# Squaring the input two adaLN rows earlier, with GpSimd summing the squares, and zeros copied from DRAM

## The chip, the cores and the metric

The kernel runs on one core of a Trainium2 chip. The core has five engines with instruction streams of their own: TensorE (PE in the rows, PEld its weight loads, PEq its sequencer), VectorE (DVE), ScalarE (ACT), GpSimd (POOL) and SyncE (SP). They meet only through semaphores. DMAs are issued by SP, ACT and POOL and are carried out by 16 DMA engines. The metric is the device time of one execution, in microseconds (us), the median of several runs.

## The reference

One inference step of a two-layer backbone, batch 1: 128 context tokens and 256 latent tokens (T = 384) of width D = 1024, in float32. Ahead of each sub-layer stands an adaLN norm; both token kinds have their own shift, scale and gate, which come from a conditioning vector and one large matrix:

```
mod = silu(cond) @ w_ada[l] + b_ada[l]        # 6 x D columns: sh1 sc1 gt1 sh2 sc2 gt2
h   = rms_norm(x, g) * (1 + sc) + sh          # rms_norm: x * rsqrt(mean(x^2) + eps) * g
```

Layer 0 then projects `h` to the inputs of a Mamba-2 scan (16 heads) and of latent attention (8 heads); layer 1 to grouped-query attention (16 heads). Each layer ends with a mixture of 16 experts, top 2 per token. The kernel returns the tokens and the new states and caches.

## The kernel before

Everything lies transposed: `xT` and `hT` are 128 partitions x 8 chunks (DC) x 384 tokens, chunk c holding channels 128c to 128c+127. Weights come in 114 slots of 128 x 3072 floats (1536 KB each, `w_d`), which SP loads one after the other into a ring of 8 buffers (L384); a buffer is loaded anew when its user has counted `slot_used` up. The order of the slots is the order of use: 6 of the first layer's adaLN (N_FIRST), 7 of the first input projection (INE), the other 26 adaLN slots that are used here and there up to the attention, the output projection, the experts. SP puts the input `xT` behind the third slot (L386) and the constants `small` (3147.5 KB, the rest of them; the first 192 KB go by ACT's queue at the very start) behind the sixth (L388). The first 8 slots wait for nothing, so all of this is queued in the first microseconds and lands in this order.

The order of work on each engine is written out by hand. The start of the program is this:

- PE, `ada(n)` for n = 0 to 5 (L438): row n of the adaLN product, 8 matmuls with a 32-column weight (16 passes in the trace, since each float32 matmul shows as two). ACT copies the row out (`copy_row`, L1028), and PE turns it into columns (`turn_row`, L450: 3 matmuls of 2 columns, 6 passes), one row behind. After row 5 both remaining rows are turned, and `ada_done` is set.
- Ahead of row 5, ACT squares the 8 chunks of x into hT (L895), PE sums them over channels with 8 matmuls against a matrix of ones (`sum_squares`, L466), ACT takes the root (L878, with a table load), and DVE the reciprocal (L1239).
- DVE adds the bias to the turned columns (`modulation`, L1233), forms g * (1 + scale) (L1246), and scales the 8 chunks in 16 instructions (L1251); ACT adds the shift (L906), chunk by chunk; PE's next matmuls take the chunks as they come (`h_chunk`).
- These next matmuls are `dk` (L677): a 48-column projection that gives dt and the rotary key. Its weights are in `small`. Then come the INE slots (L474), 8 matmuls (16 passes) for each of 13 column chunks and then for the z parts; behind column chunk 0 PE turns `dk` (`dkT`, L690), which DVE copied out. ACT and DVE run the convolution on chunks 0 to 9 in PE's shadow.
- GpSimd fills the DRAM table of expert rows (8192 rows of 4 KB) with zeros: it clears 1024 columns of the SBUF region `oTm` (L1663), waits for the eighth scaled chunk (`h_scaled`), and issues 16 DMAs of 2048 KB from there (L1667). `oTm` is later overwritten by the scan, so DVE waits for `row_cleared` ahead of the scan. GpSimd waits for it too, ahead of its sums for the second norm (`sum_chunks`, L1658), in which it adds squares of chunks 0 to 6 on the way, so that PE needs two matmuls instead of eight. That scheme is used for the norms ahead of the experts only. The small outputs kpe and ckv go by GpSimd's queue behind the zeros, and ACT and DVE wait for them at the start of the latent attention.

PSUM results go through 5 banks in turn, in the order of a list of jobs; a job's bank must have been emptied five jobs later.

Of the kernel before, what the change touches and what calls it, by code (L numbers as in the profile page):

```python
# [22 lines left out]
P = 128  # L23
D = 1024
# [16 lines left out]
N_ADA, N_INE, N_OUTE, N_MOE, N_INO, N_OUTO = 16, 7, 4, 32, 4, 3  # L41
S_ADA0 = 0
N_FIRST = 6
S_INE = S_ADA0 + N_FIRST
S_ADA_LATE = S_INE + N_INE
S_OUTE = S_ADA_LATE + 2 * N_ADA - N_FIRST
# [28 lines left out]
def build(nc, small_d, x_d, w_d, y_d, stf_d, stb_d, ckv_d, kpe_d, gk_d, gv_d):  # L75
# [7 lines left out]
    with ctx:  # L83
# [22 lines left out]
        def region(base, *widths):  # L106
# [14 lines left out]
        zs, xc, oTy, oTm, lat, dk, e_sm = region(0, 3072, CONV_C * 385, 3072, 1536, 1152, 144, 1000)  # L121
        TAIL = 3072 + CONV_C * 385 + 3072 + 1536 + 1152 + 144 + 1000
        rn, _, sq_acc = region(TAIL, 384, 116, 384)
        mod_row = [U[:, TAIL + 896:TAIL + 1280], U[:, TAIL + 500:TAIL + 884]]
        xr = [region(TAIL + 387 * i, 387)[0] for i in range(2)]
        zs3 = zs.rearrange("p (t n) -> p t n", t=NT)
# [73 lines left out]
            row_copied qkv_ready rt_exp flags_ready chosen_ready rows_ready cleared row_cleared scattered  # L200
# [40 lines left out]
        for l in range(DEPTH):  # L241
            job(("ss", l, 0), "A")
            if l == 0:
                job(("dk",), "D")
                for c in range(CONV_C):
                    job(("xbc", c), "A")
                    if c == 0:
                        job(("dkT",), "D")
                for c in range(3):
                    job(("lat", c), "D")  # L250
                for i in range(3):
                    for t in range(NT):
                        job(("z", i, t), "A")
                job(("cum",), "D")
                job(("tot",), "D")
                job(("sl", 0), "A")
                job(("sl", 1), "A")
                for i, (t, full) in enumerate(STEPS):
                    job(("xt", i, 0), "A")
                    job(("xt", i, 1), "A")  # L260
                    job(("bt", i), "A")
                    if full:
                        job(("g", i, 0), "A")
                        job(("g", i, 1), "A")
                        for u in range(8):
                            job(("bc", i, u), "D")
                        if t:
                            for d in range(2):
                                for g in range(2):
                                    job(("off", i, d, g), "D")  # L270
                        job(("yT", i, 0), "A")
                        job(("yT", i, 1), "A")
                    for d in STATES[i]:
                        job(("st", i, d), "D")
                for k in range(N_PREP + 1):
                    for hh in range(2):
                        if k < N_PREP:
                            job(("qkv", k, hh), "A")
                    for hh in range(2):
                        if k:  # L280
                            job(("qkT", k - 1, hh), "A")
                attention_jobs("mla", HM)
            else:
                for i in range(NT + 1):
                    for s in range(N_INO):
                        if i < NT:
                            job(("in", s, ORDER[i]), "A" if s % 2 else "D")
                    if i == 0:
                        job(("gkT", 3), "A")
                    if i:  # L290
                        job(("gqT", ORDER[i - 1], 0), "A")
                        job(("gqT", ORDER[i - 1], 1), "A")
                        job(("gkT", ORDER[i - 1]), "A")
                attention_jobs("gqa", HQ)
            for c in range(DC):
# [59 lines left out]
        def _(sp):  # L355
# [14 lines left out]
            for n in range(N_SLOTS):  # L370
# [13 lines left out]
                sp.dma_start(buffers[IN_BUFFER[n]], w_d[row_of_slot(n), :, :]).then_inc(slot_full[IN_BUFFER[n]], 16)  # L384
                if n == 2:
                    sp.dma_start(xT[:, :, :], x_d).then_inc(S["in_x"], 16)  # L386
                if n == N_FIRST - 1:
                    sp.dma_start(small[:, N_SMALL_FIRST:], small_d[:, N_SMALL_FIRST:]).then_inc(S["in_small"], 16)  # L388
            for c in (0, DC // 2):
                sp.wait_ge(S["x_new"], 3 * DC + c + DC // 2)  # L390
# [6 lines left out]
        def _(pe):  # L397
# [57 lines left out]

            def sum_squares(l, i):
                b = fill("ss", l, i)
                if i:
                    pe.wait_ge(S["sq_sum"], (DC - 2) * (l + 1))
                    mm(b[:, 0:T], ones, sq_acc, start=True, stop=False)  # L460
                    pe.wait_ge(S["sq_ready"], DC * (2 * l + 2))
                    filled(mm(b[:, 0:T], ones, hT[:, DC - 1, :], start=False, stop=True))
                    return
                for k in range(DC):
# [200 lines left out]

            pe.wait_ge(S["in_first"], 16)
            for n in range(N_FIRST):
                if n == N_FIRST - 1:
                    sum_squares(0, 0)
                ada(n)  # L670

            pe.wait_ge(S["in_small"], 16)
            wdk = sm("w_dk").rearrange("p (k n) -> p k n", k=DC)
            b = fill("dk")
            for k in range(DC):
                h_chunk(0, 0, k)
                ins = mm(b[0:48, 0:T], wdk[:, k, :], hT[:, k, :], start=(k == 0), stop=(k == DC - 1))  # L677
            filled(ins)
            for s in range(N_INE):
                w = slot(S_INE + s).rearrange("p (k n) -> p k n", k=DC)  # L680
                for m in range(3):
                    c = 3 * s + m
                    if c < 13:
                        b = fill("xbc", c) if c < CONV_C else fill("lat", c - CONV_C)
                        filled(project("in", b[:, 0:T], lambda k: w[:, k, P * m:P * m + P], lambda k: hT[:, k, :]))
                    if c == 0:
# [165 lines left out]
        def _(act):  # L852
# [34 lines left out]
                shift(l, i)  # L887

            def root_mean_square(l, i):
                for c in range(DC):  # L890
# [4 lines left out]
                    A(hT[:, c, :], xT[:, c, :], ACT.Square).then_inc(S["sq_ready"], 1)  # L895
                b = take("ss", l, i)
                root(rn, b[:, 0:T], D).then_inc(S["r_ready"], 1)
                act.wait_ge(S["r_ready"], 2 * l + i + 1)
# [133 lines left out]
                    copy_row(n)  # L1032

            for n in range(N_FIRST):
                if n == N_FIRST - 1:
                    root_mean_square(0, 0)
                copy_row(n)
            shift(0, 0)
            act.wait_ge(S["in_small"], 16)
# [153 lines left out]
        def _(dve):  # L1193
# [264 lines left out]
            normaliser(0, 0)  # L1458
            modulation(0)
            norm(0, 0)  # L1460
            dve.wait_ge(S["in_small"], 16)
# [6 lines left out]
            b = take("dk")  # L1468
            dve.tensor_copy(dk_f, b[0:48, 0:T]).then_inc(S["dk_by_feature"], 1)
            dve.wait_ge(S["dk_by_feature"], 1)  # L1470
            dve.sem_inc(S["free_dve"], 1)
            b = take("dkT")
            emptied_by(dve.tensor_copy(dk, b[:, 0:144]))
            dve.wait_ge(S["free_dve"], emptied[index[("dkT",)]][1])
            dve.sem_inc(S["dk_copied"], 1)
            cw = sm("conv_w")
            for c in range(CONV_C):
                dve.wait_ge(S["xr_ready"], c + 1)
                r, o = xr[c % 2], xc3[:, c, :]
                link(ts(o, r[:, 1:386], cw[:, CONV_C + c:CONV_C + c + 1], None, MUL))  # L1480
# [35 lines left out]
                ins = stt(latT[:, c, :], latT[:, c, :], g, lr[c // 2], MUL, MUL)  # L1516
            ins.then_inc(S["latn_ready"], 1)

            dve.wait_ge(S["row_cleared"], 16 * (NE * CAP // 512))
            nfull = 0  # L1520
            for i, (t, full) in enumerate(STEPS):
                dve.wait_ge(S["xtok_ready"], i + 1)
# [126 lines left out]

        @block.gpsimd  # L1650
        def _(pool):
            def sum_chunks(l):

                for c in range(1, DC - 1):
                    pool.wait_ge(S["sq_ready"], DC * (2 * l + 1) + c + 1)
                    if c > 1:
                        pool.wait_ge(S["sq_sum"], (DC - 2) * l + c - 1)
                    pool.tensor_tensor(sq_acc, hT[:, 0, :] if c == 1 else sq_acc, hT[:, c, :], ADD).then_inc(S["sq_sum"], 1)  # L1658

            def clear_rows():  # L1660

                zero = oTm[:, 0:D]
                pool.memset(zero, 0.0).then_inc(S["cleared"], 1)  # L1663
                pool.wait_ge(S["cleared"], 1)
                pool.wait_ge(S["h_scaled"], DC)
                for n in range(NE * CAP // 512):
                    pool.dma_start(rows_d[512 * n:512 * n + 512, :].rearrange("(p q) n -> p q n", q=4),  # L1667
# [2 lines left out]
            def moe(l):  # L1670
# [42 lines left out]
            sum_chunks(0)  # L1713
# [4 lines left out]
            sum_chunks(1)  # L1718
            moe(1)


# [96 lines left out]
```

## Time and profile before

| | us |
|---|---|
| median of 3 runs | 1145.91 |
| lowest and highest | 1140.90 and 1149.15 |
| the profiled execution | 1145.72 |
| its span in the trace | 1143.9 |

The page gives shares over the whole span: PE is busy 83% of it, DVE 33%, ACT 25%, POOL 4%. The change touches the first tenth of the span and one DMA stream, so those shares say little; the views to read are the timeline of the first 70 us, the chain of waits there, and the landing of single DMAs. In the rows, "x16" counts instructions merged into one row, the first column of a timeline or a chain is the start in us from the span's start, and the second the time in us.

### The profile page before, as it was taken

To read this page: it belongs to the slowest core of one execution; us is meant where nothing else is said; L and a number is where in the kernel's file an instruction comes from. 1 tells how busy PE (TensorE), PEld (TensorE's weight loads), DVE (VectorE), ACT (ScalarE), POOL (GpSimd) and SP (SyncE) were. 2 spreads that over 40 slices of the span, in tenths; PEclk is the share of its full clock that TensorE was granted. 3 is DMA by queue.
4 is the path that set the end of the run, shared out by engine and by line. 5 is a ranking of instruction groups with operands and counts; after the bars stand their busy time and mean duration, and the time that the engine had idled before them with its cause. 6 is when DMAs were issued, how large, how long until landed. Compare 5 with 4: busy or idle time off the path is not lost.

```text
span 1143.9 us, 14055 instructions
## 1 busy us (share of the span) xinstructions
PE 950.7 (83%) x5625; PEld 507.9 (44%) x5625; DVE 371.8 (33%) x924; ACT 290.7 (25%) x684; POOL 50.2 (4%) x63
## 2 busy tenths in 40 slices
PE   5999988786876699972999995898898963999994
PEld 2455655564643445532433334464544533323324
DVE  0332006655734471133111102345664151101112
ACT  1421023232333371031111110312665041101110
POOL 0310000000000000102000001000000102000002
PEclk8799998968988799986999998899789985999997
DMA  9999997532374401123599996406000216599934
GB/s 385 426 423 415 408 419 295 207 136 111 130 272 171 165 1 56 66 100 135 229 410 414 415 426 223 177 1 220 10 1 1 93 73 247 220 416 425 424 126 184
DMA packets 36339, 258.99 MB, mean 226 GB/s; under 512 B 3408, under 2 KB 3552, under 8 KB 21424
## 3 DMA queue, kind: packets, MB, share of 16 engines
q1 hardware_dynamic: 20448, 198.27, 43.3%
q0 software_dynamic: 12224, 47.01, 10.4%
q10 hardware_dynamic: 3600, 12.78, 2.8%
q8 instruction: 47, 0.77, 0.3%
q14 instruction: 20, 0.16, 0.0%
HBM read 203.17 MB, written 54.87 MB: 226 GB/s over the span
## 4 chain that ended last, share of the span: by engine, by line
PE 70%; DVE 12%; DMA 7%; ACT 6%; issue 3%; POOL 1%; SPq 0%; DVEq 0%; POOLq 0%; ACTq 0%
PE ps L474 20%; PE ps L586 13%; PE ps L608 7%; PE ps L828 6%; DMA U<-expert_rows 3%; PE ps L488 3%; PE ps L570 2%; PE ps L661 2%; PE ps L438 2%; DMA ring<-w_in 2%; PE ps L747 2%; PE ps L513 2%; PE ps L495 1%; PE ps L534 1%; DVE U L1538 1%
## 5 line engine op out<-in xcount | busy, mean ns | idle before, releaser
L586 PE MATMUL ps<-ring,U 128*32 128x512 f32 x1200 | 166.3, 592 | 0.0
L474 PE MATMUL ps<-U,ring 128*128 128x384 f32 x320 | 105.1, 487 | 2.7 <-DVE U L1317 1.4
L608 PE MATMUL ps<-ring,U 128*32 128x512 f32 x672 | 85.7, 594 | 0.0
L586 PEld LDWEIGHTS ps<-ring,U 128*32 128x32 f32 x1200 | 47.5, 110 | 85.3 <-issue 85.3
L474 PEld LDWEIGHTS ps<-U,ring 128*128 128x128 f32 x320 | 60.0, 189 | 47.4 <-issue 4.2
L586 PE MATMUL ps<-U 128*32 128x512 f32 x168 | 73.1, 592 | 0.0
L586 PE MATMUL ps<-hT,U 128*32 128x512 f32 x168 | 73.1, 592 | 0.0
L438 PE MATMUL ps<-ring,cond_w 128*32 128x384 f32 x512 | 59.5, 592 | 14.4 <-ACT cond_w L883 8.6
L828 PE MATMUL ps<-ring,hT 128*128 128x384 f32 x192 | 65.4, 501 | 5.7 <-ACT hT L906 4.9
L474 PE MATMUL ps<-hT,ring 128*128 128x384 f32 x208 | 68.6, 488 | 1.0 <-issue 1.0
L570 PE MATMUL ps<-small,U 128*128 128x128 f32 x192 | 31.7, 317 | 44.2 <-DMA U<-expert_rows 42.4
L1400 DVE TENSOR_TENSOR U<-ps,U 128x256 f32<-128x256 f32 x24 | 10.1, 422 | 134.7 <-ACT U L974 134.7
L474 PEld LDWEIGHTS ps<-hT,ring 128*128 128x128 f32 x208 | 39.0, 190 | 30.0 <-issue 4.0
L488 PE MATMUL ps<-U,hT 64*128 64x128 f32 (+3 forms) x144 | 50.0, 524 | 2.5 <-ACTq L924 1.1
L828 PEld LDWEIGHTS ps<-ring,hT 128*128 128x128 f32 x192 | 37.1, 196 | 33.1 <-issue 9.2
L570 PEld LDWEIGHTS ps<-small,U 128*128 128x128 f32 x192 | 24.4, 161 | 54.2 <-DMA U<-expert_rows 48.2
L895 ACT ACTIVATE hT<-xT 128x384 f32<-128x384 f32 x32 | 15.3, 517 | 129.5 <-DVE xT L1259 105.7
L1408 DVE COPY U<-ps 128x512 f32<-128x512 f32 x24 | 16.6, 692 | 91.6 <-PE ps L608 56.4
L661 PE MATMUL ps<-U 128*128 128x128 f32 x192 | 26.1, 306 | 23.5 <-DMA U<-expert_rows,U 23.5
L1259 DVE SCALAR_TENSOR_TENSOR xT<-ps,misc,xT 128x128 f32<-128x128 f32 (+1 forms) x32 | 11.9, 413 | 96.0 <-PE ps L474 96.0
L974 ACT ACTIVATE U<-ps 128x256 f32<-128x256 f32 x24 | 9.2, 385 | 131.2 <-PE ps L586 131.2
L474 PE MATMUL ps<-ring,hT 128*128 128x384 f32 (+1 forms) x144 | 42.0, 451 | 0.5 <-issue 0.5
(250 smaller groups left out, 1346.6 us busy)
## 6 DMA issues: line engine op xcount, KB each, us to landing
ring<-w_in SPq DMA_DIRECT2D x102, 1536.0 KB, 10.6
expert_rows<-U POOLq DMA_DIRECT2D x16, 2048.0 KB, 70.9
U<-expert_rows SPq DMA_DIRECT2D x24, 512.0 KB, 5.9
expert_rows<-U ACTq DMA_DIRECT2D x24, 512.0 KB, 9.0
hT<-w_in SPq DMA_DIRECT2D x6, 1536.0 KB, 12.2
U<-w_in SPq DMA_DIRECT2D x6, 1536.0 KB, 15.6
small<-small_in SPq DMA_DIRECT2D x1, 3147.5 KB, 34.1
xT<-x_in SPq DMA_DIRECT2D x1, 1536.0 KB, 16.7
```

Source lines behind the costliest of these rows:

```text
L438: ins = mm(ps[q:q + 32, bank_row, 0:384], cond3[:, k, :], w[:, k, :], start=(k < 4), stop=(k >= 4))
L474: ins = mm(out, lhs(k), rhs(k), start=(k == 0), stop=(k == n - 1))
L488: filled(mm(b[:, 0:nk], q_of(t, h), k_of(h, k0, nk), start=True, stop=True))
L513: ins = mm(ps[rows[i], 5 + pair % 2, P:T], v_of(1 + c, 2 * k + i), pt[i][:, P + 256 * c:P + 256 * c + 256], start=(c == 0), stop=(c == NT ...
L570: ins = pe.transpose(ps[:, 3 + h, P * c:P * c + P], xgb[i % NR][:, 512 * h + P * c:512 * h + P * c + P], ident)
L586: ins = mm(ps[q:q + 32, r, :], xgT[:, r, P * k + q:P * k + q + 32], w[e][:, c:c + 512], start=(k == 0), stop=(k == DC - 1))
L608: ins = mm(ps[q:q + 32, 6 + h, :], actT_of[i % NR][:, P * j + q:P * j + q + 32], w[e][:, c:c + 512], start=(j == 0), stop=(j == 1))
L661: ins = mm(ps[:, MIX_BANK[t] + h, P * c:P * c + P], picked[t][q][:, 512 * h + P * c:512 * h + P * c + P], gate_diag[q][t], start=(q == 0), ...
L747: ins = mm(ps[:, 5 + q // 2, 64 * hh:64 * hh + 64], dec[u % 3][:, P * h:P * h + P], xdt[d][:, 64 * (4 * q + h):64 * (4 * q + h) + 64], sta ...
L828: ins = mm(b[:, 0:384], hT[:, k, TILE[t]], w[:, k, :], start=(k == 0), stop=(k == DC - 1))
L895: A(hT[:, c, :], xT[:, c, :], ACT.Square).then_inc(S["sq_ready"], 1)
L1408: dve.tensor_copy(ysb[i % 2][:, 512:1024], ps[:, 7, :]).then_inc(S["y_dve"], 1)
```

## The change

1. ACT's root_mean_square(0, 0) is cut in two: the squares come ahead of `copy_row(3)`, the root ahead of `copy_row(4)`. PE's `sum_squares(0, 0)` moves from ahead of `ada(5)` to ahead of `ada(4)`.
2. The first norm uses GpSimd's sums as the expert norms do: GpSimd adds the squares of chunks 0 to 6 into `sq_acc0` (in the region oTy, free by then), six additions; PE does two matmuls.
3. SP loads the seventh slot (the first of INE) ahead of `small`.
4. `dk` moves behind column chunk 5 of INE, `dkT` behind chunk 6; the first INE column chunk now takes the chunks of h as they come. PE's wait for `small` moves along; DVE's moves behind the memsets of the convolution's edges; ACT's stays behind the shift.
5. The zeros are read from DRAM: the last output slot of layer 1 fills only 2048 of its 3072 columns, and the 1024 padded ones are the source. The memset and DVE's wait for `row_cleared` go.

```diff
+N_SQUARE = 3
+DK_AFTER = 5
...
+        sq_acc0 = oTy[:, 0:T]
...
-                if n == N_FIRST - 1:
+                if n == N_FIRST:
                     sp.dma_start(small[:, N_SMALL_FIRST:], small_d[:, N_SMALL_FIRST:]).then_inc(S["in_small"], 16)
...
             def sum_squares(l, i):
                 b = fill("ss", l, i)
-                if i:
-                    pe.wait_ge(S["sq_sum"], (DC - 2) * (l + 1))
-                    mm(b[:, 0:T], ones, sq_acc, start=True, stop=False)
-                    pe.wait_ge(S["sq_ready"], DC * (2 * l + 2))
+                if i or not l:
+                    pe.wait_ge(S["sq_sum"], (DC - 2) * (l + i + 1))
+                    mm(b[:, 0:T], ones, sq_acc if i else sq_acc0, start=True, stop=False)
+                    pe.wait_ge(S["sq_ready"], DC * (2 * l + i + 1))
...
             for n in range(N_FIRST):
-                if n == N_FIRST - 1:
+                if n == N_SQUARE + 1:
                     sum_squares(0, 0)
                 ada(n)
...
-            pe.wait_ge(S["in_small"], 16)
-            b = fill("dk")
-            for k in range(DC):
-                h_chunk(0, 0, k)
-                ins = mm(b[0:48, 0:T], wdk[:, k, :], hT[:, k, :], start=(k == 0), stop=(k == DC - 1))
-            filled(ins)
...
+                    if c == DK_AFTER:
+                        pe.wait_ge(S["in_small"], 16)
+                        b = fill("dk")
+                        filled(project("dk", b[0:48, 0:T], lambda k: wdk[:, k, :], lambda k: hT[:, k, :]))
+                    if c == DK_AFTER + 1:
                         pe.wait_ge(S["dk_by_feature"], 1)
...
             for n in range(N_FIRST):
-                if n == N_FIRST - 1:
-                    root_mean_square(0, 0)
+                if n == N_SQUARE:
+                    squares(0, 0)
+                if n == N_SQUARE + 1:
+                    root_of(0, 0)
                 copy_row(n)
...
-            dve.wait_ge(S["row_cleared"], 16 * (NE * CAP // 512))
...
-                zero = oTm[:, 0:D]
-                pool.memset(zero, 0.0).then_inc(S["cleared"], 1)
-                pool.wait_ge(S["cleared"], 1)
+                zero = w_d[S_OUTO + 2, :, 2 * D:SLOT]
...
+            sum_chunks(0, 0)
             clear_rows()
```

On PE, this is the start of the program from the fourth adaLN row on (`ring<-cond_w` rows are adaLN rows, `misc,U` the turns), before:

```order
L438 MATMUL ps<-ring,cond_w 32x384 x8
L450 MATMUL ps<-misc,U 128x2 x3
L438 MATMUL ps<-ring,cond_w 32x384 x8
L450 MATMUL ps<-misc,U 128x2 x3
L466 MATMUL ps<-hT,small 128x384 x8
L438 MATMUL ps<-ring,cond_w 32x384 x8
L450 MATMUL ps<-misc,U 128x2 x6
L677 MATMUL ps<-hT,small 48x384 x8
L474 MATMUL ps<-hT,ring 128x384 x8
```

And the same place now:

```order
L442 MATMUL ps<-ring,cond_w 32x384 x8
L454 MATMUL ps<-misc,U 128x2 x3
L464 MATMUL ps<-U,small 128x384
L466 MATMUL ps<-hT,small 128x384
L442 MATMUL ps<-ring,cond_w 32x384 x8
L454 MATMUL ps<-misc,U 128x2 x3
L442 MATMUL ps<-ring,cond_w 32x384 x8
L454 MATMUL ps<-misc,U 128x2 x6
L686 MATMUL ps<-hT,ring 128x384 x8
L478 MATMUL ps<-hT,ring 128x384 x40
L478 MATMUL ps<-hT,small 48x384 x8
```

Eight sum matmuls became two and stand one row earlier; the 48-column projection went behind 48 matmuls of the input projection.

On GpSimd, from its first own instruction to the outputs of layer 0 (U holds the zeros before; `ISA` ahead of an addition sets up the engine for it), before:

```order
L1663 MEMSET U 128x1024
L1667 DMA expert_rows<-U 512x1x1024 x16
L1706 DMA kpe_out<-U 128x32
L1708 DMA stf_out<-small 128x512
L1709 DMA stb_out<-small 128x512
L1711 DMA ckv_out<-U 128x128
L1658 ISA
L1658 TENSOR_TENSOR U<-hT 128x384
```

And now:

```order
L1675 ISA
L1675 TENSOR_TENSOR U<-hT 128x384
L1675 TENSOR_TENSOR U<-U,hT 128x384 x5
L1682 DMA expert_rows<-w_in 512x1x1024 x16
L1722 DMA kpe_out<-U 128x32
```

The additions and their set-up stand first, and the 16 zeroing DMAs now go from DRAM to DRAM.

## Rows read from the trace of the kernel before

**Rows 1.** The page: chain's share by engine, and DMA busy tenths in 40 slices.
```profile
PE 70%; DVE 12%; DMA 7%; ACT 6%; issue 3%; POOL 1%; SPq 0%; DVEq 0%; POOLq 0%; ACTq 0%
...
DMA  9999997532374401123599996406000216599934
```
**Rows 2.** Chain of waits in order of time, first 57 us: start, us, what.
```profile
3.06 19.72 DMA ring<-w_in
...
22.82 2.79 PE ps L438 x16
25.61 1.37 PE ps L450 x6
26.98 2.71 PE ps L438 x16
...
31.07 7.37 PE ps L466 x16
...
39.05 2.57 DVE U L1239
...
41.64 0.21 DVE misc L1233
...
43.81 7.80 PE ps L677 x16
51.61 5.36 PE ps L474 x16
```
**Rows 3.** Timeline, 0 to 70 us: start, us, engine, line, instructions.
```profile
30.23 3.41 ACT L895 ACTIVATE hT<-xT 128x384 f32<-128x384 f32 x8
...
38.35 1.50 PE L438 MATMUL ps<-ring,cond_w 128*32 128x384 f32 x16
...
39.78 1.59 PE L450 MATMUL ps<-misc,U 128*128 128x2 f32 x12
...
42.09 5.36 DVE L1251 SCALAR_TENSOR_TENSOR hT<-xT,misc,U 128x128 f32<-128x128 f32 x16
42.87 5.63 ACT L906 ACTIVATE hT<-hT,misc 128x128 f32<-128x128 f32 x16 [2.38 <-DVE hT L1251]
```
**Rows 4.** Stretches: busy us (x instructions) by engine, then granted clock, DMA share, GB/s.
```profile
31.00:35.00 4.00, 4.00 (x8) 2.18 (x8) 0.00 (x0) 3.92 (x8) 0.00 (x0) 0.50 1.03 441
...
36.00:38.40 2.40, 2.40 (x12) 1.19 (x14) 0.00 (x0) 0.00 (x0) 0.00 (x0) 1.00 0.90 380
...
43.80:48.80 5.00, 4.99 (x8) 1.63 (x9) 4.00 (x17) 4.70 (x14) 0.66 (x1) 0.50 1.02 430
```
**Rows 5.** DMAs issued at 2.36, 4.2, 4.62 and 5.13 us: KB, us to landing.
```profile
xT<-x_in SPq DMA_DIRECT2D x1, 1536.0 KB, 16.7
...
ring<-w_in SPq DMA_DIRECT2D x1, 1536.0 KB, 26.0
...
small<-small_in SPq DMA_DIRECT2D x1, 3147.5 KB, 34.1
...
ring<-w_in SPq DMA_DIRECT2D x1, 1536.0 KB, 37.3
```
**Rows 6.** GpSimd's groups of instructions: busy us, mean ns, idle before them.
```profile
L1658 POOL TENSOR_TENSOR U<-U,hT 128x384 f32<-128x384 f32 x10 | 8.6, 864 | 58.1 <-ACT hT L895 58.1
...
L1658 POOL TENSOR_TENSOR U<-hT 128x384 f32<-128x384 f32 x2 | 2.0, 988 | 211.6 <-ACT hT L895 211.6
```
**Rows 7.** Timeline further on: SP's loads, input projection, scan, late adaLN row, GpSimd.
```profile
67.88 325.27 SPq L384 DMA_DIRECT2D ring<-w_in  x33
...
68.07 15.72 PE L474 MATMUL ps<-hT,ring 128*128 128x384 f32 x48 [0.26 <-issue]
...
183.67 1.22 DVE L1574 TENSOR_TENSOR U<-hT,U 128x1024 f32<-128x1024 f32 x1
...
219.46 1.50 PE L438 MATMUL ps<-ring,cond_w 128*32 128x384 f32 x16
...
453.20 0.99 POOL L1658 TENSOR_TENSOR U<-hT 128x384 f32<-128x384 f32 x1 [124.77 <-ACT hT L895]
```
**Rows 8.** DMA, 48 to 180 us: GpSimd's queue (q0) and SP's (q1).
```profile
q0 software_dynamic: 8480, 33.57, 62.4%
q1 hardware_dynamic: 1876, 20.46, 37.7%
```
**Rows 9.** Zeroing DMAs: landing min/median/max; then the slot issued between 165 and 172 us.
```profile
DMA to landing us min/median/max: 23.5/70.9/121.6
...
ring<-w_in SPq DMA_DIRECT2D x1, 1536.0 KB, 12.4
```
**Rows 10.** Chain of waits, whole span: the first matmuls of the latent attention.
```profile
397.67 6.29 PE ps L488 x12
```

More of the change, by code:

```diff
@@ L199, in build @@
             qt_copied qk_sq qk_r qk_ready qkT_ready max_ready e_ready p_ready pt_ready pv_done o_ready x_new row_done
-            row_copied qkv_ready rt_exp flags_ready chosen_ready rows_ready cleared row_cleared scattered
+            row_copied qkv_ready rt_exp flags_ready chosen_ready rows_ready row_cleared scattered
             turned0 turned1 xgT_act xgT_dve up_done sil_ready act_ready act_turned actT_ready down0 down1 y_act y_dve
@@ L243, in build @@
             if l == 0:
-                job(("dk",), "D")
                 for c in range(CONV_C):
                     job(("xbc", c), "A")
-                    if c == 0:
+                    if c == DK_AFTER:
+                        job(("dk",), "D")
+                    if c == DK_AFTER + 1:
                         job(("dkT",), "D")
@@ L684, in _ @@
                         b = fill("xbc", c) if c < CONV_C else fill("lat", c - CONV_C)
-                        filled(project("in", b[:, 0:T], lambda k: w[:, k, P * m:P * m + P], lambda k: hT[:, k, :]))
-                    if c == 0:
+                        if c == 0:
+                            for k in range(DC):
+                                h_chunk(0, 0, k)
+                                ins = mm(b[:, 0:T], w[:, k, 0:P], hT[:, k, :], start=(k == 0), stop=(k == DC - 1))
+                            filled(ins)
+                        else:
+                            filled(project("in", b[:, 0:T], lambda k: w[:, k, P * m:P * m + P], lambda k: hT[:, k, :]))
+                    if c == DK_AFTER:
+                        pe.wait_ge(S["in_small"], 16)
+                        b = fill("dk")
+                        filled(project("dk", b[0:48, 0:T], lambda k: wdk[:, k, :], lambda k: hT[:, k, :]))
+                    if c == DK_AFTER + 1:
                         pe.wait_ge(S["dk_by_feature"], 1)
@@ L889, in root_mean_square, with squares @@
             def root_mean_square(l, i):
+                squares(l, i)
+                root_of(l, i)
+            def squares(l, i):
                 for c in range(DC):
@@ L895, in root_mean_square, with root_of @@
                     A(hT[:, c, :], xT[:, c, :], ACT.Square).then_inc(S["sq_ready"], 1)
+            def root_of(l, i):
                 b = take("ss", l, i)
@@ L1460, in _ @@
             norm(0, 0)
-            dve.wait_ge(S["in_small"], 16)
             dve.wait_ge(S["h_scaled"], DC)
@@ L1466, in _ @@
             dve.sem_inc(S["xr_used"], 1)
[L1468 to L1475, printed above, removed]
             cw = sm("conv_w")
+            dve.wait_ge(S["in_small"], 16)
             for c in range(CONV_C):
+                if c == DK_AFTER + 1:
+                    b = take("dk")
+                    dve.tensor_copy(dk_f, b[0:48, 0:T]).then_inc(S["dk_by_feature"], 1)
+                    dve.wait_ge(S["dk_by_feature"], 1)
+                    dve.sem_inc(S["free_dve"], 1)
+                    b = take("dkT")
+                    emptied_by(dve.tensor_copy(dk, b[:, 0:144]))
+                    dve.wait_ge(S["free_dve"], emptied[index[("dkT",)]][1])
+                    dve.sem_inc(S["dk_copied"], 1)
                 dve.wait_ge(S["xr_ready"], c + 1)
@@ L1651, in _, with sum_chunks @@
         def _(pool):
-            def sum_chunks(l):
+            def sum_chunks(l, i):
+                acc = sq_acc if i else sq_acc0
                 for c in range(1, DC - 1):
-                    pool.wait_ge(S["sq_ready"], DC * (2 * l + 1) + c + 1)
+                    pool.wait_ge(S["sq_ready"], DC * (2 * l + i) + c + 1)
                     if c > 1:
-                        pool.wait_ge(S["sq_sum"], (DC - 2) * l + c - 1)
-                    pool.tensor_tensor(sq_acc, hT[:, 0, :] if c == 1 else sq_acc, hT[:, c, :], ADD).then_inc(S["sq_sum"], 1)
+                        pool.wait_ge(S["sq_sum"], (DC - 2) * (l + i) + c - 1)
+                    pool.tensor_tensor(acc, hT[:, 0, :] if c == 1 else acc, hT[:, c, :], ADD).then_inc(S["sq_sum"], 1)
             def clear_rows():
-                zero = oTm[:, 0:D]
-                pool.memset(zero, 0.0).then_inc(S["cleared"], 1)
-                pool.wait_ge(S["cleared"], 1)
+                zero = w_d[S_OUTO + 2, :, 2 * D:SLOT]
                 pool.wait_ge(S["h_scaled"], DC)
@@ L1712, in _ @@
             pool.wait_ge(S["row_cleared"], 16 * (NE * CAP // 512))
-            sum_chunks(0)
+            sum_chunks(0, 1)
             moe(0)
@@ L1717, in _ @@
             pool.dma_start(gv_d, qkv3[:, 0, 1280:1536]).then_inc(outs["gv"], 16)
-            sum_chunks(1)
+            sum_chunks(1, 1)
             moe(1)
```

## The prediction

> **What bounds the kernel now.** I read the page first, for which engine the chain runs through: 70% of the chain is PE, and the DMA engines are busy all the time in the first slices [rows 1]. So a change is worth what it takes off PE's path, and a transfer matters only where it lands late. Then the chain in the first 57 us [rows 2], for what really stands one behind the other there. The reader is to see four stages: the fourth adaLN slot is waited for until 22.78 us; then PE works without a gap up to 38.44 (row 3, turn, row 4, turn, the sums of squares); then root, reciprocal, bias and scaling lie on the path, the bias of the modulation starting at 41.64; and at 43.81 PE has its first chunk of h. From there it is PE alone: 16 passes of dk until 51.61, the input projection, 15.72 us for each of its slots [rows 2, 7]. Third, the timeline for what is idle beside this [rows 3]: ACT squares x at 30.23 only, though x, issued at 2.36, had landed 16.7 us later, at 19.06 [rows 5]. Fourth, the granted clock [rows 4]: 0.50 (the 1.2 GHz level) in 31 to 35 us, where PE summed, 1.00 (2.4 GHz) from 36 on, and 0.50 again in 43.8 to 48.8, after PE had stood idle for 2.4 us. The same adaLN row takes 2.79 us at the low level and 1.50 at the high one [rows 2, 3].
>
> The profiled execution took 1145.72 us, the median of the runs shown is 1145.91: the sum is made against 1145.7.
>
> **The squares and sums (the term that counts).** ACT can square from 19.06 on; 3.41 us for the eight [rows 3] ends at 22.5, before row 3 of adaLN is done at 25.6, so row 3's copy is not held up. GpSimd's six additions take 0.99 and five times 0.864 [rows 6], 5.3 us; from the second square (about 19.9) on that ends at 25.2. PE comes to the sums at 26.98, where row 4 started before [rows 2]: 1.8 us of slack, or 0.3 for each addition's wait for the one before. The sums are now 4 passes instead of 16. At the low clock a pass of 384 columns takes 0.64 us: 31.07 to about 35.6 is seven of them, the other nine go at 0.32 and end at 38.44 [rows 2, 4]. Four low passes make 2.56: PE is free at 29.54. Root (0.5) and reciprocal (2.57) then end at about 32.7, beside row 4 and long before the modulation: they leave the path.
>
> Behind that stand row 4, a turn, row 5 and two turns. The sixth slot, issued at about 4.2, lands 26.0 later, at 30.2 [rows 5], and is no limit. What it costs hangs on the clock, which the trace of before cannot show for this order:
> - Never up before the modulation: 2.79 and 1.37 for row 4 and its turn, 33.7; then row 5 and both turns at 2.71 + 2.74 + 0.3 for the last copy: modulation at 39.5, 2.1 earlier than now.
> - Up as soon as the sums are done: 1.50 and 0.80, 31.8; from the start of row 5 to the modulation it took 3.29 at the high clock (38.35 to 41.64) [rows 2, 3]: 35.1, 6.5 earlier.
> - Up at the end of row 4: 29.54 + 2.79 + 0.80 + 3.29 = 36.4, 5.2 earlier.
>
> Before, the clock was low through rows 3 and 4 with their turns and came up inside the sums, the first work there without a turn in between; sums and row 4 are such work now. I take the third, which also lies between the others: **5.2 us**.
>
> **Scaling and first projection.** From 41.64 to PE's first chunk at 43.81 nothing is altered (2.17 us), so PE starts at about 38.6. Its slot, the seventh, is now ahead of `small`: before it landed at 5.13 + 37.3 = 42.4, behind `small` at 38.7 [rows 5]; the difference is its own 3.7 us, so it lands at 30.2 + 3.7 = 33.9, in time. Without this edit the early start would be lost to the slot. The 16 passes paced by the chunks take 7.80 as dk's did [rows 2]. If the clock stays up over the gap, ACT's 5.63 for the shift [rows 3] sets the pace, 2.4 less; if it does not come up within the stretch, 16 passes at 0.64 are 2.4 more. I take 0, the row's own value.
>
> **dk behind chunk 5.** The same 16 passes, now 5.2 us at the high clock, in a stage where PE never waits; DVE has copied it out while PE does chunk 6 (5.2 us), so dkT does not wait. Its first reader on the path is the scan, a hundred us on. Zero. `small` now lands at 42.4; ACT, which waits for it behind the shift (over at 42.87 + 5.63 - 5.2 = 43.3), and DVE need it no earlier.
>
> **Zeros from DRAM.** The removed wait of DVE: the last zeroing DMA, issued at 57.7, landed 121.6 later, at 179.3 [rows 9]; DVE went on to the scan at 183.67 right after other work [rows 7]. Worth nothing before; with the scan 5 us earlier it would just have held, so it is not a gain but a hold-up avoided. The transfer itself: 33.57 MB took 62.4% of the 16 engines over 132 us, 82.4 us of them [rows 8]. No row shows DRAM to DRAM. Least is that it stays so, most by the nearest rows that reading costs as much again as SP's loads, 49.8 us for 20.46 MB [rows 8]: 82 more, 164 in all. Either way it is hidden: they start behind the eighth scaled chunk, at 42.09 + 5.36 = 47.45 before [rows 3], 42.3 now; the slot issued at about 168 landed in 12.4 us and was used at 219.46 [rows 7, 9], so a load may take four times as long. The next reader of the zeros is GpSimd at 453 [rows 7]. I take zero, and the lower end, since the bytes written are the same.
>
> The Trainium skill, "DMA: Bandwidth & Descriptors", Latency and other measured facts, speaks against this edit: it gives copies from HBM to HBM 214 GB/s per direction at a good row pitch, where the rows here show 407 for the zeros from SBUF. By it the zeros would take an estimated 157 us of the engines instead of 82, inside the bounds above, and the sum would stay as it is. No run here shows it yet; it raises the chance of the third rival a little.
>
> **Sum:** 1145.7 - 5.2 = **1140.5 us**.
>
> **Rivals.**
>
> *1. The clock stays low* through row 5. For: rows 3 and 4 of adaLN with their turns ran low from 22.8 to 31 [rows 2], and there are fewer dense passes now. Against: the unbroken run is still there. Gain 2.1: 1143.6.
>
> *2. GpSimd is late.* Its set-up and first addition now stand at the head of the program. For: PE waits in order, so every us beyond the slack of 1.8 goes to rows 4 and 5 as well, one to one. Against: the first addition took 0.988 in both layers, with the set-up in front or not [rows 6], and the others 0.864; but in layer 0 it had stood idle for 124.77 us [rows 7], now some 18. At 7.0 us late the gain is gone, beyond it the kernel is slower. I price it at additions of twice their row, 5.3 more, 3.5 past the slack: 1144.0. The Trainium skill, "GPSIMD Engine Reference", 2.1 Instruction dispatch, states about 6 us for the first call of freshly loaded code; paid at the call that would be 4.2 us past the slack, an estimated 1144.7; paid from the set-up on it is hidden. This trace shows no such 6 us.
>
> *3. The zeros hold the queue (slower).* kpe and ckv go out behind them on the same queue, and ACT and DVE wait for both at the start of the latent attention, 397.67 before [rows 10], 392.5 now. SP loads 33 slots from 67.88 to 393 and some 7 more land after 43 [rows 7]: 40 times 1.573 MB at the 411 GB/s of [rows 8] is 153 us of the engines. That leaves 392.5 - 42.3 - 153 = 197 for the zeros, 2.4 times their price now. Beyond that all of the rest waits: at three times (247 us) they end at 442, and the kernel takes 1140.5 + 50 = 1190. Against: it needs more than reading and writing one after the other.
>
> **How the numbers follow.** Chances: forecast 0.64, rival 1 0.18, rival 2 0.13, rival 3 0.05. The forecast's own ends are 2.1 - 2.4 and 6.5 + 2.4, so 1137 to 1146; the three runs of before lie 5 below to 3 above their median, as the new ones will. With rivals 1 and 2 inside: 1134.5 to 1147.5. About 1% (11.5 us) is what can be told from no change here. Faster by more needs the fast ends of both clock terms and a lucky median: 0.06. Slower by more is rival 3: 0.04. Within 1%: 0.90.
>
> **What would show it.** Right: ACT's squares at 19 us; GpSimd's sixth addition done before 27; sum passes 4 in number at 27; modulation at 36 to 37, first chunk at 38 to 39 with its slot landed at 34; a gapless input projection that ends 5 us before 163.7; late adaLN rows without a DMA wait. Wrong: PE idle at the sums until GpSimd; adaLN row 5 at 2.7 us; zeros that land after 300; a shift at 60 us that is gone by 400.

## The result and the profile after

The changed kernel takes 1135.88 us (median of 12 runs, 1132.91 to 1139.77) against 1141.64 of the kernel before in 12 runs beside it (1138.45 to 1153.89). The ratio is 0.9927, with a 95% interval of 0.9899 to 0.9955: 0.73% faster, or 8.3 us of 1141.6 (5.1 to 11.5). The ratio is not that of the medians, which differ by 5.8 us only: 3 of the 12 executions of the kernel before lie above 1149 us, and none of the changed kernel's above 1140. The forecast was a gain of 5.2 us, a time of 1140.5, and, at 0.90, a change within the 1% that it took for the least that can be told. The range held the time and the change lies within 1%; but it is told from none, and by the ratio the gain lies above the forecast, with 5.2 just inside the interval.

The profiled execution took 1136.11 us, its span is 1134.5, 9.4 less than in the profile before. That one, of 1145.72 us, lay 4 us above the median of the 12, so the two traces differ by more than the medians do. The chain of waits of the changed kernel, 20 to 60 us (start, us, what), which answers to [rows 2]:

```profile
4.13 25.94 DMA ring<-w_in
...
33.26 0.20 DVE misc L1249
...
35.43 7.09 PE ps L686 x16
42.52 10.32 PE ps L478 x32
```

The modulation (the bias, with which the scaling of x begins) starts at 33.26 instead of 41.64 and PE's first chunk comes at 35.43 instead of 43.81: 8.4 us. The chain no longer runs through the sums, root and reciprocal at all, but through the sixth adaLN slot, the weights of row 5, which lands at 30.07. The timeline of the same stretch (start, us, engine, line, instructions) shows why:

```profile
19.02 3.41 ACT L907 ACTIVATE hT<-xT 128x384 f32<-128x384 f32 x8 [1.53 <-DMA xT<-x_in]
20.04 0.99 POOL L1675 TENSOR_TENSOR U<-hT 128x384 f32<-128x384 f32 x1 [19.35 <-ACT hT L907]
21.18 4.89 POOL L1675 TENSOR_TENSOR U<-U,hT 128x384 f32<-128x384 f32 x5
...
26.36 0.89 PE L464 MATMUL ps<-U,small 128*128 128x384 f32 x2
...
27.09 0.81 PE L466 MATMUL ps<-hT,small 128*128 128x384 f32 x2
...
27.82 1.50 PE L442 MATMUL ps<-ring,cond_w 128*32 128x384 f32 x16
...
30.12 1.50 PE L442 MATMUL ps<-ring,cond_w 128*32 128x384 f32 x16
```

ACT squares at 19.02, GpSimd's last addition ends at 26.07, and PE's four passes run from 26.36 to 27.8: at the high clock level, as both adaLN rows behind them (1.50 each). The stretches (busy us and instructions by engine, then the granted clock) answer to [rows 4]:

```profile
22.70:26.00 3.30, 3.26 (x19) 1.14 (x20) 0.00 (x0) 0.32 (x1) 2.87 (x4) 0.51 1.04 439
...
26.40:33.10 6.70, 6.66 (x55) 3.68 (x55) 2.55 (x1) 2.52 (x4) 0.00 (x0) 1.00 1.06 444
33.10:35.40 2.30, 0.03 (x1) 0.00 (x1) 2.07 (x8) 0.92 (x3) 0.00 (x0) 1.00 0.90 388
35.40:39.40 4.00, 3.97 (x8) 2.16 (x9) 3.80 (x14) 4.00 (x13) 0.03 (x1) 0.60 1.10 472
```

The clock came up at about 26, in the turn of row 3, before the sums and not behind row 4. From 42.52 on, 9.1 us ahead of the kernel before, nothing more is gained: DVE goes on to the scan at 174.38 instead of 183.67 [rows 7], 9.3 earlier, and the last stretch, PE's mixing of the expert rows, starts at 1115.88 instead of 1125.31, 9.4 earlier. First come the rows of the chain at the end, before and after; the timeline row behind them is DVE's at the scan, the others are the zeroing DMAs' landing and, for 39 to 171 us, the queues of GpSimd (q0) and SP (q1), as in [rows 7 to 9]:

```profile
1125.31 13.60 PE ps L661 x96
...
1115.88 13.70 PE ps L665 x96
```
```profile
174.38 1.22 DVE L1590 TENSOR_TENSOR U<-hT,U 128x1024 f32<-128x1024 f32 x1
```
```profile
DMA to landing us min/median/max: 23.8/90.5/157.0
```
```profile
q0 software_dynamic: 7043, 28.00, 57.0%
q1 hardware_dynamic: 2194, 24.05, 44.3%
```

The last zeros, issued at 49.0, land at 206 and not at 179, so 32 us after DVE has started on the region that held the zeros before. Nobody waits for them now. Per byte they cost little more than from SBUF: 28.00 MB in 57.0% of 132 us are 75.2 us of the engines, 372 GB/s against 407 before, about 90 us for all of them instead of 82.4. Where no load of SP's was in flight, from 101.3 to 106.4 us, the zeros from DRAM ran at 392 GB/s; those from SBUF ran at 421 from 111.2 to 115.7 in the trace of before.

### The profile page after: what moved, and what is told of

It is laid out like the page before. It is cut to its first block, busy times and chain, and to the rows that moved or that the text cites. A ratio compares the mean times of both kernels' runs of the same rounds, so it can differ in the third digit from the quotient of the medians.

```text
span 1134.5 us, 14040 instructions
## 1 busy us (share of the span) xinstructions
PE 941.1 (83%) x5613; PEld 503.9 (44%) x5613; DVE 371.6 (33%) x924; ACT 290.8 (26%) x684; POOL 54.3 (5%) x68
## 3 DMA queue, kind: packets, MB, share of 16 engines
q0 software_dynamic: 12224, 47.01, 11.1%
## 4 chain that ended last, share of the span: by engine, by line
PE 70%; DVE 12%; DMA 8%; ACT 6%; issue 3%; POOL 1%; SPq 0%; DVEq 0%; PEld 0%; POOLq 0%; ACTq 0%; PEldq 0%
PE ps L478 20%; PE ps L590 13%; PE ps L612 7%; PE ps L836 6%; PE ps L492 3%; DMA U<-expert_rows 3%; PE ps L574 2%; PE ps L665 2%; DMA ring<-w_in 2%; PE ps L755 2%; PE ps L517 2%; PE ps L442 1%; PE ps L499 1%; PE ps L538 1%; DVE U L1554 1%
## 5 line engine op out<-in xcount | busy, mean ns | idle before, releaser
L442 PE MATMUL ps<-ring,cond_w 128*32 128x384 f32 x512 | 57.2, 571 | 15.5 <-ACT cond_w L891 8.5
L478 PE MATMUL ps<-hT,ring 128*128 128x384 f32 x192 | 63.3, 488 | 0.9 <-issue 0.8
L1416 DVE TENSOR_TENSOR U<-ps,U 128x256 f32<-128x256 f32 x24 | 10.1, 422 | 134.9 <-ACT U L988 134.9
L478 PEld LDWEIGHTS ps<-hT,ring 128*128 128x128 f32 x192 | 36.1, 190 | 27.5 <-issue 3.3
```

The source lines that it names most:

```text
L442: ins = mm(ps[q:q + 32, bank_row, 0:384], cond3[:, k, :], w[:, k, :], start=(k < 4), stop=(k >= 4))
L478: ins = mm(out, lhs(k), rhs(k), start=(k == 0), stop=(k == n - 1))
```

## The experiments

Four theories stood against each other. The path theory: the whole gain is what the modulation and the first projection start earlier, and it needs the slot order. The clock theory: the edits are worth 5 us, and the rest is the clock that came up early. The elsewhere theory: part of the gain is made behind the front, by the zeros above all. The wait theory, formed after the first four runs: an earlier front makes DVE's wait for the zeros bite, so that removing the wait is a condition of the gain. Each ratio is to the kernel before in runs beside it, with its 95% interval; kernels of different experiments ran at different times, and where two of them are compared it is by these ratios, with the medians beside them.

**Only the early squares and GpSimd's sums** (parts 1 and 2; the diff is that of `sum_squares`, `root_mean_square` and `sum_chunks` above, with `sum_chunks(0, 0)` behind the memset's place).

> Only the early squares and GpSimd's sums (parts 1 and 2); small still lands ahead of the seventh slot, dk still first, zeros from SBUF. Path theory: the modulation starts at 33.3 as in the changed kernel (clock up) or up to 39.5 (clock low), but dk then waits for small, which lands at 38.7, so PE's first chunk is at 38.8 and the kernel gains 5 us (0.44%), not 8 or 9. Clock theory (the edits are worth 5 and the rest was a lucky clock): also about 5, but with the first chunk at 36 and no wait for small. Elsewhere theory (part of the gain comes from the zeros): under 5, and the trace after 60 us differs.

Measured: 1151.57 us, 1.0051 (1.0019 to 1.0083): slower. The path and the clock theory had a gain of 5 us; the elsewhere theory had "under 5" and a changed trace behind 60 us, which is so, but it named no loss. The front did what the path theory said; PE's timeline and then DVE's, of this kernel:

```profile
30.44 1.50 PE L440 MATMUL ps<-ring,cond_w 128*32 128x384 f32 x16 [0.26 <-DMA ring<-w_in]
31.87 1.59 PE L452 MATMUL ps<-misc,U 128*128 128x2 f32 x12
38.82 7.33 PE L679 MATMUL ps<-hT,small 128*48 128x384 f32 x16 [5.36 <-DMA small<-small_in]
```
```profile
176.61 1.68 DVE L1526 SCALAR_TENSOR_TENSOR U<-U,small,hT 128x384 f32<-128x384 f32 x3
188.38 1.23 DVE L1584 TENSOR_TENSOR U<-hT,U 128x1024 f32<-128x1024 f32 x1 [10.10 <-DMA expert_rows<-U]
```

The landing of this kernel's zeroing DMAs (the last was issued at 49.7), and SP's loads issued from 140 to 179 us, before and then here:

```profile
DMA to landing us min/median/max: 23.8/80.9/138.7
```
```profile
ring<-w_in SPq DMA_DIRECT2D x4, 1536.0 KB, 10.4
...
ring<-w_in SPq DMA_DIRECT2D x6, 1536.0 KB, 12.2
```

dk waits 5.36 us for `small` and starts at 38.82, 5 us early, as expected. But at the scan DVE, ready at 178.3, stands 10.1 us for the zeros from SBUF, which landed at 179.3 before and at 188.4 here. The DMA engines are busy in both traces nearly all the time from 140 us on, before until about 176, here until the zeros are through. 4 of SP's loads were issued in 140 to 179 us before and 6 here, because the adaLN rows that free their buffers come earlier too: before, the loads behind those rows went out at 178.1, 181.5 and 184.5, here at 171.1, 174.2 and 177.2. From the first zeroing DMA to the landing of the last (131.2 us before, 148.3 here) SP's queue moved 20.33 MB before and 28.25 MB here. At the 417 GB/s of both queues together in that stretch the 7.9 MB more are an estimated 19 us, where the zeros took 17.1 longer.

**Only the slot order and the moved dk** (parts 3 and 4).

> Only the slot order and the moved dk (parts 3 and 4). Path theory: nothing, within 0.5 us, since before neither small (38.7) nor the seventh slot (42.4) was waited for at 43.81 and dk's 16 passes only change place; first chunk at 43.8 as before. Elsewhere theory: a gain of 1 us or more. Clock theory: nothing.

Measured: 1148.69 us, 1.0022 (0.9987 to 1.0057): no difference that can be told. Against the expectation the first chunk came at 40.08, since the clock came up ahead of row 4 in this profile (modulation at 37.91, though up to there PE's work is in the order of the kernel before), and DVE stands at the same wait, 11.1 us; the span is 1152.0:

```profile
190.09 1.23 DVE L1589 TENSOR_TENSOR U<-hT,U 128x1024 f32<-128x1024 f32 x1 [11.08 <-DMA expert_rows<-U]
```

**Only the zeros from DRAM** (part 5).

> Only the zeros from DRAM, with the memset and DVE's wait gone (part 5). Path theory: nothing, within 0.5 us: the zeros take 90 instead of 82 us of the DMA engines and land about 25 us later, and nobody waits. Elsewhere theory: 1 to 4 us faster, in the scan. Clock theory: nothing.

Measured: 1140.78 us, 0.9979 (0.9953 to 1.0004); the runs reach from 1139.1 to 1145.9 where those of the kernel before beside them reach to 1152.9, 13 of 35 above 1146. That is the picture of a wait that bites in some executions only, and 2.4 us by the ratio would fit the elsewhere theory's 1 to 4; but the interval takes in 1.

**Eight sum matmuls at the early place, without GpSimd:**

```
-                if i or not l:
-                    pe.wait_ge(S["sq_sum"], (DC - 2) * (l + i + 1))
+                if i:
+                    pe.wait_ge(S["sq_sum"], (DC - 2) * (l + 1))
...
-            sum_chunks(0, 0)
```

> The changed kernel without GpSimd's sums: PE adds the squares of all 8 chunks with 8 matmuls, at the new place ahead of row 4. Path theory: 16 passes from 26.4 on, at the high clock 5.2 us, so row 4 starts at 31.7 instead of 27.8 and the modulation at 37.1 instead of 33.3: 3.8 us of the gain are lost (more where part of it is at the low clock). Clock theory (the clock made the gain, not the fewer passes): the long run of passes keeps the clock up and under 1.5 us are lost.

Measured: 1140.15 us, 0.9962 (0.9935 to 0.9989): by the ratios 4.0 us of the gain are gone, about half, as the path theory said (3.8); the two intervals overlap. PE's timeline:

```profile
26.84 7.67 PE L470 MATMUL ps<-hT,small 128*128 128x384 f32 x16
34.44 1.50 PE L442 MATMUL ps<-ring,cond_w 128*32 128x384 f32 x16
```

The sixteen passes took 7.67 us here (5.43 at the high level in another trace, that of the slot order alone; so about 7 of them ran at the low one), row 4 starts 6.6 us later than in the changed kernel's trace and the first chunk comes at 41.94. So the early place alone is not the gain; without a second engine the sums push row 4 back.

**The changed kernel with zeros from SBUF again** (the memset, DVE's wait and the source back, all else kept):

```
-                zero = w_d[S_OUTO + 2, :, 2 * D:SLOT]
+                zero = oTm[:, 0:D]
+                pool.memset(zero, 0.0).then_inc(S["cleared"], 1)
+                pool.wait_ge(S["cleared"], 1)
...
+            dve.wait_ge(S["row_cleared"], 16 * (NE * CAP // 512))
             nfull = 0
```

> The changed kernel with its zeros from SBUF again: memset, and DVE's wait for the landing ahead of the scan. Wait theory (the earlier front makes that wait bite, as in the two runs with part of the front, where DVE stood 10.1 and 11.1 us): the front as in the changed kernel, DVE ready for the scan at about 174.5, the zeros landed at 188 to 190, so 13 to 15 us of waiting: slower than before by 3 to 6 us, slower than the changed kernel by 12 or more. Theory of the prediction (the wait is worth nothing): as fast as the changed kernel, within 1 us.

Measured: 1151.98 us, 1.0041 (1.0014 to 1.0067): slower than before, and 13 us (by the ratios) to 16 us (by the medians) slower than the changed kernel, which did not run beside it. DVE's timeline and PE's:

```profile
174.03 1.68 DVE L1533 SCALAR_TENSOR_TENSOR U<-U,small,hT 128x384 f32<-128x384 f32 x3
191.38 1.23 DVE L1591 TENSOR_TENSOR U<-hT,U 128x1024 f32<-128x1024 f32 x1 [15.68 <-DMA expert_rows<-U]
```
```profile
29.78 1.87 PE L442 MATMUL ps<-ring,cond_w 128*32 128x384 f32 x16
...
37.65 6.97 PE L686 MATMUL ps<-hT,ring 128*128 128x384 f32 x16 [2.30 <-ACT hT L920]
```

This is what the wait theory expected. DVE waits 15.7 us, and the whole loss is there; the row names the zeroing DMAs, though source and wait were changed back together. This front also shows the changed kernel's other course: the clock came up within row 4 (1.87 us), and the first chunk came at 37.65, 6.2 us early and not 8.4.

**`small` ahead of the seventh slot again** (`if n == N_FIRST - 1:` in the changed kernel).

> The changed kernel with small ahead of the seventh slot again. Path theory: the slot lands at 42.4 instead of 34, so the first projection starts there and not at 35.4; its chunks are all ready by then, it ends at 48 to 49 instead of 42.5: 6 us of the changed kernel's gain are lost, some 3 remain. Rival (the DMA order does not matter since the later work makes up for it): within 1 us of the changed kernel.

Measured: 1141.65 us, 0.9955 (0.993 to 0.9979). PE's timeline:

```profile
42.33 4.04 PE L686 MATMUL ps<-hT,ring 128*128 128x384 f32 x6 [9.24 <-DMA ring<-w_in]
```

PE stands 9.24 us for its slot. In the trace 6.9 us of the front are lost (42.33 instead of 35.43); from the changed kernel, which did not run beside it, the ratios differ by 3.2 us and the medians by 5.8. The order of two DMAs, which together with dk's place is worth nothing that can be told, seems to carry a good part of the gain once the sums are early and dk stands behind; the two intervals overlap.

**Needless matmuls in both gaps of PE**, in the changed kernel (`keep_busy(6, 7)` is 7 matmuls of 128x384, ones times constants, into bank 6, results unused):

```
...
+                if n == 3:
+                    keep_busy(6, 7)
...
+            keep_busy(5, 3)
```

> The changed kernel with needless matmuls on PE in its two idle gaps (7 of 128x384 ahead of row 3, 3 behind the last turn; results unused). Landing theory (the modulation is now bound by the sixth slot, which lands at 30.1): the modulation stays at 33.3; the first projection runs at the high clock from its start and is paced by ACT, ending at 40.8 instead of 42.5: 1.7 us faster than the changed kernel's profile. Clock theory (the changed kernel's runs differ by where the clock comes up at the start): 2 to 5 us in the median of the runs, and a narrower spread.

Measured: 1134.66 us over 6 runs, 0.9895 (0.986 to 0.993). The first projection takes 5.66 us, as expected, but PE came to the sums so early that it waited 1.15 us for GpSimd; the clock fell meanwhile, and row 5 started 1.3 us later than in the changed kernel's trace:

```profile
26.14 1.46 PE L464 MATMUL ps<-U,small 128*128 128x384 f32 x2 [1.15 <-POOL U L1682]
```

The landing theory was right on the projection and wrong in that the modulation stays put. Against the changed kernel it is 3.7 us by the ratios and 1.2 by the medians, with intervals that overlap.

**The same ahead of row 3, in the kernel before:**

> The kernel before with the 7 needless matmuls ahead of row 3, and nothing else. Clock theory: rows 3 and 4 and the sums run at the high level, the modulation starts at 36 instead of 41.6, PE's first chunk at 38.2. Wait theory on top of it: the scan still waits for the zeros, which land at 185 to 190, so of the 5.6 us nothing is left at the scan, and the kernel is as fast as before or up to 5 us slower. Without the wait theory: 5.6 us faster.

Measured: 1148.35 us, 1.0001 (0.9969 to 1.0034). Rows 3 and 4 and the sums ran high, the modulation started at 37.81, 3.8 us early and not 5.6 (row 4 now waited 1.43 us for its slot and the sums for ACT's squares), and at the scan it was taken back:

```profile
184.32 1.23 DVE L1580 TENSOR_TENSOR U<-hT,U 128x1024 f32<-128x1024 f32 x1 [4.36 <-DMA expert_rows<-U]
```

DVE starts at 184.32, where it started at 183.67 without the clock's help. 5 of SP's loads were issued in 140 to 179 us. So with the wait in place, a clock that comes up early is enough to make it bite.

**Sums and zeros, without slot order and dk** (the first run with part 5 added).

> The early squares with GpSimd's sums and the zeros from DRAM without DVE's wait; slot order and dk as before. Wait theory: dk starts when small lands, at 38.8 instead of 43.8, and now nothing at the scan takes the 5 us back: 4.5 to 6 us faster than before, the changed kernel 3 to 4 us faster still. Rival (the early sums are slower for a reason of their own, as the run with them alone could be read): no faster than the run with the zeros alone, 0.2% under before.

Measured: 1138.73 us, 0.9938 (0.9906 to 0.997), 7.1 us under before (one of the 12 executions took 1229.95 us; nothing here says why). The run with the sums alone had been 0.51% slower. Part 5, the zeros from DRAM with the wait gone, makes the difference between the two, and the early sums are not slow of themselves. PE's timeline:

```profile
38.67 7.71 PE L679 MATMUL ps<-hT,small 128*48 128x384 f32 x14 [3.12 <-DMA small<-small_in]
```

The gain is more than the 4.5 to 6 us expected, and the 3 to 4 us that the changed kernel was to have beyond it were not found: it has 1.3 us more by the ratios, whose intervals overlap, and 2.9 by the medians. What parts 3 and 4 are worth together, beside the other parts, is thus not shown.

**Needless matmuls and zeros from DRAM, in the kernel before.**

> The kernel before with the 7 needless matmuls ahead of row 3 and the zeros from DRAM without DVE's wait. Wait theory: the modulation at 37.8, 3.8 us earlier than in the trace of before, and all of it is kept: 3 to 5 us under the run with the zeros alone (some 5 to 7 under before). Rival (the clock at the start is worth nothing to the end, as the run with needless matmuls alone could be read): as the run with the zeros alone.

Measured: 1140.12 us, 0.9956 (0.9928 to 0.9984), 5.0 us. In this profile the clock fell again ahead of row 4, and the modulation started at 40.47, only 1.2 early; against the zeros alone (0.9979) it is 2.6 us, and the intervals overlap. What the clock is worth by itself stays open; the aim of 3 to 5 us beyond the zeros was not shown.

**Needless matmuls in the second gap only**, in the changed kernel.

> The changed kernel with 3 needless matmuls on PE behind the last turn only. If PE's clock falls in that gap in most runs: the first projection takes 5.6 instead of 7.1 us and the kernel is 1 to 1.7 us faster than the changed one, near 1134. Rival (the needless matmuls delay PE's first chunk as much as they save): the same time.

Measured: 1133.56 us over 10 runs, 0.9902 (0.9868 to 0.9936). PE's timeline:

```profile
35.43 2.20 PE L676 MATMUL ps<-small 128*128 128x384 f32 x6
37.64 5.66 PE L688 MATMUL ps<-hT,ring 128*128 128x384 f32 x16
```

The granted clock of that projection is in the last column but two:

```profile
37.60:43.20 5.60, 5.58 (x18) 2.65 (x18) 4.03 (x17) 4.73 (x14) 1.61 (x3) 1.00 0.94 399
```

The first chunk came at 37.64, where the run with zeros from SBUF, whose rows 3 to 5 ran alike, had it at 37.65: nothing is delayed, and 6.97 became 5.66. It is 1.3 us in the trace; by the medians, not taken side by side, 2.3. The intervals of this and of the changed kernel overlap, so it is the likely best, not a proven one.

**The kernel before, profiled once more.**

> The kernel before, profiled once more. Wait theory: the landing of the last zeros moves from run to run, and this run either shows DVE waiting for them ahead of the scan by 1 to 10 us, or lands them within 5 us of the time at which DVE is ready. Theory of the prediction: DVE never waits there.

Measured: 1143.82 us. The last zeros were issued at 58.0 and landed 121.9 later, at 179.9; DVE went on at 183.99, without waiting:

```profile
183.99 1.22 DVE L1574 TENSOR_TENSOR U<-hT,U 128x1024 f32<-128x1024 f32 x1
```

So in both traces of the kernel before the wait is missed by 4 us. That it bites in this kernel's executions above 1146 (8 of the 27 beside these last runs) is argued and not seen in a trace of it. For it speak the run with the zeros alone, whose front is that of the kernel before and of whose 12 executions none is above 1146, and the run with needless matmuls, where an early clock alone made the wait bite.

## Where the prediction failed, and what of it held

Two steps failed. The term for squares and sums was mis-sized (5.2 us, where the traces show 6 to 8), and the wait that part 5 removes was priced at nothing, where it decides between gain and loss. With them fell the call that the change would not be told from none.

- **Squares and sums.** The mechanism held in every part: squares at 19, sums of four passes at 26 to 27, root and reciprocal off the path, and the run with eight passes lost about half of the gain, with intervals that overlap. The size failed: "I take the third: 5.2 us". The traces show the modulation 8.4 us early where the clock came up ahead of the sums (changed kernel) and the first chunk 6.2 early where it came up in row 4 (zeros from SBUF). Nothing in the traces says which course a run takes, so for the forecast it is luck. Over all of them the modulation starts at 41.64, 41.93, 41.47 and 37.91 with the old order of PE's work (the kernel before twice, zeros alone, slot order alone) and at 33.26, 33.59, 33.22, 35.49, 35.67 and 35.48 with the new one (changed kernel, sums alone, `small` first, zeros from SBUF, sums and zeros, second gap): 40.7 and 34.5 on average, so 6.3 us, and the 8.4 of the first pair is the lucky end. My choice among the three cases rested on one trace, where the clock came up in the sums, "the first work there without a turn in between"; in the changed kernel it came up in a turn. The upper case, 6.5, was no bound: it let the sums themselves run low, and their start at 26.98 counted a turn at the low level. The true bound was in [rows 5]: the sixth slot lands at 30.2, and 3.29 behind that is 33.5. I had written that this slot is no limit; where the clock is up by the sums, it is the limit that the chain now runs through.
- **Slot and first projection.** The seventh slot landed in time, but at 35.02 and not 33.9, only 0.4 us ahead of the first chunk. With dk moved but without the slot's new place 3.2 us (ratios, overlapping) to 5.8 (medians) are lost, as the step said; with dk too at its old place, where it waits 3.12 us for `small`, it is 1.3 to 2.9. The projection took 7.09 and 6.97 instead of 7.80, a term set to 0 that is worth 0.7 to 0.8.
- **dk behind chunk 5** cost nothing: the input projection stayed without a wait.
- **Zeros from DRAM.** The transfer was hidden, as said, and near the lower bound. The failed step is the price of the removed wait: "worth nothing before; with the scan 5 us earlier it would just have held". I took the landing at 179.3 as fixed. It is not: an earlier front frees buffers earlier, two more of SP's loads share the engines before the zeros are through, and they land at 184 to 191. The wait then takes 4 to 16 us, as much as the front gains or more. Removing it is therefore no zero but the condition of the whole gain: 1.0051 becomes 0.9938 with part 5, and 0.9927 becomes 1.0041 without. By the ratio the gain is 3 us above the forecast, by the medians 0.6. How much of that is the wait in the kernel before (0.2% by the run with the zeros alone, with an interval up to no effect) and how much the front stays open.
- **The Trainium skill's rate for HBM copies** ("DMA: Bandwidth & Descriptors", Latency and other measured facts, 214 GB/s per direction): the zeros here went beyond it, with 372 GB/s by the engines' share and 392 where they ran alone, and the measurement decides. Their rows and their queue are others than those of the copies behind that figure, so it is not shown wrong for those.
- **Rivals.** A clock low through row 5 was seen in no trace: row 5 took 1.50 in all of them. GpSimd was not late: its first addition took 0.99 us, 19 us behind its set-up, and PE waited for it only where needless matmuls had brought PE there early. So the six microseconds of the Trainium skill, "GPSIMD Engine Reference", 2.1 Instruction dispatch, did not show at the call. The zeros did not hold the queue: they ended at 206, and the latent attention began at 388.42 against 397.67 [rows 10]. The mechanism that could turn the kernel slower was among none of the rivals, since it lay in the wait that this change removes: it is what a part of the change alone meets.

## What to carry to other kernels

Ask of every wait that holds by a few microseconds what sets its release, and whether that moves against the work when the work gets earlier: here a bulk transfer on shared DMA engines landed later when an earlier front issued more loads. An edit that is worth nothing that can be told by itself (here a removed wait) can be the condition of the one that pays, so price it with the others in place. And for the upper end of a gain go to the next thing that must arrive, not to the fastest case that one had in mind for the engine.

## What was not expected of the hardware

DRAM to DRAM at 4 KB rows cost the DMA engines 90 us for 33.6 MB, only 9% more than SBUF to DRAM (82.4); where they ran alone it was 392 GB/s against 421. And three needless matmuls, 2.20 us in an idle gap of 2.3, kept PE's granted clock at 1.00, where it was 0.50 to 0.58 from 36 to 39 us in the changed kernel's trace: the 16 passes behind them took 5.66 us instead of 6.97 to 7.09, about as long as ACT took for its shifts (5.64).
